# Filter spectra split by token modulo four, two items moved to the first choice of tokens, and mean squares ahead of the layers' barrier

## The reference, cut to what matters

```python
mod = (silu(cond) @ mod_w + mod_b)              # shift, scale, gate, twice: 6 x 1024 a layer
h = rms_norm(x, norm1_w) * (1 + sc1) + sh1
# filters, of the positions alone
h = sin(z @ w1 + b1); h = sin(h @ w2 + b2); h = (h @ w3 + b3) * window
# Hyena: twice
z = parts[o + 1] * bidir_fftconv(z, filt[:, 0, o], filt[:, 1, o], bias[o])   # irfft(rfft(z) * rfft(filt))
x = x + g1 * (merged @ w_o)
h2 = rms_norm(x, norm2_w) * (1 + sc2) + sh2
aff = softmax(h2 @ router_w); gate, idx = top_k(aff.T, cap)   # each of 16 experts chooses its tokens
x = x + g2 * sum over experts of (silu(xs @ w_gate) * (xs @ w_up)) @ w_down * gate
```

## Time and profile before

| | us |
|---|---|
| median of 3 runs | 2148.35 (2147.32 to 2151.87) |
| profiled execution | 2155.39 |
| its span | 2153.6 |

### The profile page before, as it was taken

One profiled execution on the slowest core, in us unless ns is written; L12 is line 12 of the kernel. 1 busy time (PEld: TensorE's weight loads), 2 busy tenths in 40 slices (PEclk: granted clock), 3 DMA queues, 4 the chain that ended last, 5 costly groups with the idle time before them and its releaser, 6 DMA issues.

```text
span 2153.6 us, 35885 instructions
## 1 busy us (share of the span) xinstructions
PE 2095.7 (97%) x13286; PEld 1707.6 (79%) x13286; DVE 1681.4 (78%) x2516; ACT 1134.5 (53%) x1798; POOL 164.2 (8%) x192
## 2 busy tenths in 40 slices
PE   8999999999999999999999999999999999999999
PEld 3449999998768997666668999999766999666666
DVE  7767878876768645999997787887777764799997
ACT  5434444324712255888884444433651225788884
POOL 1110000001001100111100000000100100111110
PEclk9999999999999999999999999999999999999999
DMA  9982433213133517999992243222413434999995
GB/s 334 329 305 87 147 136 119 83 75 117 76 118 136 171 62 294 392 382 385 382 354 98 96 147 133 98 82 76 152 42 135 159 130 159 353 378 385 385 386 216
DMA packets 76975, 435.80 MB, mean 202 GB/s; under 512 B 9228, under 2 KB 9900, under 8 KB 36381
## 3 DMA queue, kind: packets, MB, share of 16 engines
q1 hardware_dynamic: 54336, 352.87, 42.7%
q0 software_dynamic: 19024, 72.32, 10.7%
q10 hardware_dynamic: 3470, 8.64, 1.1%
HBM read 384.95 MB, written 48.84 MB: 201 GB/s over the span
## 4 chain that ended last, share of the span: by engine, by line
PE 80%; DVE 8%; ACT 4%; issue 4%; DVEq 2%; DMA 2%; ACTq 0%; POOL 0%; another core or an unknown queue 0%; POOLq 0%
PE ps L738 21%; PE ps L977 17%; PE ps L1322 9%; PE ps L1348 5%; PE ps L1326 4%; PE ps L919 3%; PE ps L1352 2%; PE ps L843 2%; PE ps L1049 2%; DMA kspec<-back 2%; PE ps L777 2%; PE ps L1174 2%; PE ps L1177 1%; PE ps L933 1%; PE ps L1102 1%
## 5 line engine op out<-in xcount | busy, mean ns | idle before, releaser
L738 PE MATMUL ps<-front_r 128*128 128x320 f32 x2432 | 417.0, 310 | 1.6 <-DVE back_r L2474 0.8
L738 PEld LDWEIGHTS ps<-front_r 128*128 128x128 f32 x2432 | 370.1, 188 | 3.0 <-DVE back_r L2474 1.4
L1420 ACT ACTIVATE front_r<-ring 128x1024 fp32r<-128x1024 f32 (+1 forms) x216 | 182.5, 845 | 261.2 <-PE ps L738 172.1
L977 PE MATMUL ps<-back_r,front_r 128*128 128x320 f32 x1728 | 265.1, 309 | 0.0
L977 PEld LDWEIGHTS ps<-back_r,front_r 128*128 128x128 f32 x1728 | 256.4, 188 | 0.0
L1420 ACT ACTIVATE back<-ps 128x512 f32<-128x512 f32 (+5 forms) x206 | 98.5, 496 | 249.6 <-PE ps L738 114.1
L977 PE MATMUL ps<-front_r 128*128 128x320 f32 x1296 | 204.7, 311 | 5.3 <-DVE back L2153 5.1
L977 PEld LDWEIGHTS ps<-front_r 128*128 128x128 f32 x1296 | 191.9, 188 | 10.4 <-DVE back L2153 9.5
L1420 ACT ACTIVATE front_r<-back 128x512 fp32r<-128x512 f32 (+2 forms) x216 | 150.1, 709 | 87.8 <-PE ps L977 35.0
L2588 DVE TENSOR_TENSOR back_r<-front,back_r 128x1024 fp32r<-128x1024 f32 x128 | 153.5, 1220 | 12.4 <-ACT back_r L1420 10.6
L1322 PE MATMUL ps<-back_r 128*80 128x512 f32 x384 | 152.3, 397 | 3.7 <-ACT back_r L1420 3.7
(11 more groups left out here) (317 smaller groups left out, 3734.8 us busy)
## 6 DMA issues: line engine op xcount, KB each, us to landing
ring<-in_stream SPq DMA_DIRECT2D x186, 1024.0 KB, 7.9
front<-in_stream SPq DMA_DIRECT2D x80, 1024.0 KB, 16.0
back<-in_stream SPq DMA_DIRECT2D x48, 1024.0 KB, 14.9
gates<-back SPq DMA_DIRECT2D x24, 640.0 KB, 3.1
back<-gates POOLq DMA_DIRECT2D x48, 320.0 KB, 3.3
kspec<-back POOLq DMA_DIRECT2D x20, 512.0 KB, 8.4
front<-kspec POOLq DMA_DIRECT2D x8, 1024.0 KB, 7.7
rows<-front ACTq DMA_DIRECT2D x10, 520.0 KB, 5.4
```

The lines of the kernel that those rows point to most:

```text
L738: mm = pe.matmul(tokh(b)[:, c0:c1], w(wp)[:, k, :], src(hp, k)[:, c0:c1], start=first, stop=last)
L977: mm = pe.matmul(ps[:, bank, 0:TH], w[:, wp, k, :], x(k), start=k == 0 and wp == 0 and x is hi and j not in (2, 6), stop=k == 3 and wp == ...
L1420: return act.activation(o, i, ACT.Copy)
```

## The change

- **Spectra.** Latent tokens are ordered by 0, 2, 1, 3 modulo 4 in effect: the even half is itself made of a transform of tokens 0 and one of tokens 2 modulo 4, over 128 frequencies only (two matmuls for each of the two parts), whose sum and difference are the even halves for kt = 0 and 1 (`keven`); the odd half stays two matmuls each. ACT copies one of the two (`ktwo`) and the prompt's spectrum; the copies of odd halves go. PE, ACT and DVE now wait for one another within a step through banks 0 to 3 of PSUM.
- **Items.** `LATE` becomes ((5, 6), (6, 4)), so `EARLY` is 27; `STEPS` tells how many a step does. In the choice of tokens three items come ahead of the transposes of the places, the others behind them, and then 4 (layer 0) or 10 (layer 1) matmuls into a bank that nobody reads. SP issues expert loads 0 to 2 instead of 0 to 5 ahead of its wait for the gather.
- **Router's shift.** `router_shift` comes behind `inverse(1)`, with one matmul that transposes the shift's columns; ACT and DVE split the result into `shift_rows`. `diag` and its 16 scalings a layer go; DVE makes `spread_rows` with two products of 96 x 1024 in the output projection and a low part of `spr`, and `add_shift` is one fp32r matmul of 512 columns over 96 partitions.
- **Between the layers.** Mean squares and root come ahead of the barrier, with 6 filler matmuls on PE.

The diff, cut to its core:

```diff
-MODS, LATE = DEPTH * N_MOD, ((5, 4), (6, 4))
+MODS, LATE = DEPTH * N_MOD, ((5, 6), (6, 4))
 EARLY = MODS - sum(sum(n) for n in LATE)
...
+        STEPS = (1,) * 10 + (1, 2, 1, 2, 2) + (1, 1, 2, 1, 2)
         def step_mods(n):
-            first = [2 + min(x, 10) + (EARLY - 12) * max(x - 10, 0) // 10 for x in (n, n + 1)]
-            return tuple(range(*first))
+            first = 2 + sum(STEPS[:n])
+            return tuple(range(first, first + STEPS[n]))
...
                 for x in range(LAP):
-                    if x == 6:
+                    if x == 3:
...
                 unit, u = n // 5, n % 5
-                b = 2 * (n % 2)
                 pe.wait_ge(f_tapsread, 5 * unit + 5)
-                if n >= 2:
-                    wait_spectrum(pe, n - 2)
                 if u == 0:
+                    pe.wait_ge(k_evac, 4 * unit)
                     for r in range(2):
-                        mm = pe.matmul(ps[:, b + r, :], cfi[:, r, :], (fa, fb)[r][:, unit % 2, 0, :],
+                        mm = pe.matmul(ps[:, r, :], cfi[:, r, :], (fa, fb)[r][:, unit % 2, 0, :], start=True, stop=True)
+                    mm.then_inc(k_ready, 1)
+                else:
+                    r, kt = (u - 1) // 2, (u - 1) % 2
+                    if r:
+                        pe.wait_ge(k_evac, 4 * unit + 1 + kt)
+                    else:
+                        pe.wait_ge(k_first, unit + 1)
+                    for t in range(2):
+                        mm = pe.matmul(ps[:, kt, :], cft[:, r, 2 + t, P * kt:P * kt + P],
+                                       (fa, fb)[r][:, unit % 2, 3 + t, :], start=t == 0, stop=t == 1)
+                    mm.then_inc(k_ready, 1)
+                if u in (0, 2):
+                    r = u // 2
+                    if unit or r:
+                        pe.wait_ge(k_evac, 4 * unit + 1 if r else 4 * unit - 1)
+                    for t in range(2):
+                        mm = pe.matmul(ps[:, 2 + t, :], cft[:, r, t, 0:P], (fa, fb)[r][:, unit % 2, 1 + t, :],
                                        start=True, stop=True)
-                else:
-                    kt, r = (u - 1) // 2, (u - 1) % 2
-                    for odd in (1, 0):
-                        for t in range(2):
-                            mm = pe.matmul(ps[:, b + odd, :], cft[:, r, 2 * odd + t, P * kt:P * kt + P],
-                                           (fa, fb)[r][:, unit % 2, 1 + 2 * odd + t, :], start=t == 0, stop=t == 1)
-                mm.then_inc(k_ready, 1)
+                    mm.then_inc(k_ready, 1)
...
                 if l:
-                    mean_squares(l, 0)
                     spread(l, 0)
...
                             for k in range(KC):
-                                mm = pe.matmul(ps[:, 7, 320 + NE * g:320 + NE * g + NE],
+                                pe.matmul(ps[:, 7, 320 + NE * g:320 + NE * g + NE],
                                                mod[:, l, 24 + k, g:g + 1].to_broadcast([P, P]), rw[:, k, :],
                                                start=k == 0, stop=k == KC - 1)
-                        mm.then_inc(r_lg, 1)
+                        pe.wait_ge(sh_hi, 2 * l + 1)
+                        pe.matmul(ps[:, 7, 0:P], shift_cols, ident[:], start=True, stop=True).then_inc(r_lg, 1)
...
                         prompt_forward()
+                    inverse(1, range(4))
+                    if o == 0:
                         router_shift()
-                    inverse(1, range(4))
                 prompt_inverse(1)
...
                     t, hf = n // 2, n % 2
-                    for i in range(4):
-                        mm = pe.matmul(ps[:, 4 + n % 2, P * i:P * i + P], spr[:, P * t:P * t + P],
-                                       diag[:, int(t > 0), 4 * hf + i, :], start=False, stop=i == 3)
-                    mm.then_inc(t_ready, 1)
+                    pe.matmul(ps[:, 4 + n % 2, :], spr[0:96, P * t:P * t + P],
+                              spread_rows[0:96, int(t > 0), 4 * hf:4 * hf + 4, :].rearrange("p i n -> p (i n)"),
+                              start=False, stop=True).then_inc(t_ready, 1)
...
                 mm.then_inc(r_affT, 1)
-                pe.wait_ge(z_ready, l * Z_IN + Z_IN)
+                pe.wait_ge(rt_lo, 3 * l + 3)
                 add_shift(0)
...
-                pe.wait_ge(r_places, l * 2 + 1)
-                apart(pe)
-                pe.transpose(ps[0:SLOTS, 0, 0:LISTS], places[:], ident[0:LISTS, 0:LISTS])
-                pe.transpose(ps[0:CAP[1], 0, LISTS:2 * LISTS], best[:], ident[0:LISTS, 0:LISTS]).then_inc(r_placesT, 1)
-                pe.wait_ge(numbers_in, l * 32 + 32)
-                pe.wait_ge(r_places, l * 2 + 2)
-                apart(pe)
-                seconds = turned[0:CAP[1], :].rearrange("p (a n) -> p a n", a=2)[:, :, 32:32 + NE]
-                pe.matmul(ps[0:CAP[1], 1, 0:2 * NE], flip, seconds, start=True, stop=True).then_inc(r_placesT, 1)
+                def turn_places():
+                    pe.wait_ge(r_places, l * 2 + 1)
+                    apart(pe)
+                    pe.transpose(ps[0:SLOTS, 0, 0:LISTS], places[:], ident[0:LISTS, 0:LISTS])
+                    pe.transpose(ps[0:CAP[1], 0, LISTS:2 * LISTS], best[:], ident[0:LISTS, 0:LISTS]).then_inc(r_placesT, 1)
+                    pe.wait_ge(numbers_in, l * 32 + 32)
+                    pe.wait_ge(r_places, l * 2 + 2)
+                    apart(pe)
+                    seconds = turned[0:CAP[1], :].rearrange("p (a n) -> p a n", a=2)[:, :, 32:32 + NE]
+                    pe.matmul(ps[0:CAP[1], 1, 0:2 * NE], flip, seconds, start=True, stop=True).then_inc(r_placesT, 1)
                 mods = late_mods(l, 1)
-                for i in mods:
+                for x, i in enumerate(mods):
+                    if x == 3:
+                        turn_places()
                     mod_rows(i)
-                    if i > mods[0]:
+                    if x:
                         mod_columns(i - 1)
                 mod_columns(mods[-1])
+                keep_busy(2, 10 if l else 4)
...
                     add_rows(1, m)
+                if l + 1 < DEPTH:
+                    pe.wait_ge(c_read, l * 8 + 6)
+                    keep_busy(2, 6)
+                    pe.wait_ge(c_read, l * 8 + KC)
+                    mean_squares(l + 1, 0)
                 end_phase(pe, l)
...
-            def spectrum_odd(n):
-                act.wait_ge(k_ready, n + 1)
-                b = 2 * (n % 2)
-                if n % 5:
-                    if n >= 2:
-                        wait_spectrum(act, n - 2)
-                    copy(kodd[:, n % 2, :], ps[:, b + 1, :]).then_inc(k_odd, 1)
-                else:
+            def spectrum_parts(n):
+                unit, u = n // 5, n % 5
+                if u == 0:
+                    act.wait_ge(k_ready, 7 * unit + 1)
                     if n >= 2:
                         act.wait_ge(k_stored[n % 2], 16 * (n // 2))
-                    copy(kout[:, n % 2], ps[:, b:b + 2, :]).then_inc(k_first, 1)
+                    copy(kout[:, n % 2], ps[:, 0:2, :]).then_inc(k_first, 1)
+                if u in (0, 2):
+                    act.wait_ge(k_ready, 7 * unit + (5 if u else 2))
+                    if unit or u:
+                        act.wait_ge(k_evac, 4 * unit + 1 if u else 4 * unit - 1)
+                    copy(ktwo, ps[:, 3, :]).then_inc(k_odd, 1)
...
                     if o:
+                        act.wait_ge(r_lg, 2 * l + 1)
+                        copy(shift_rows, ps[:, 7, 0:P]).then_inc(sh_hi, 1)
                         act.wait_ge(y_sum, l * 4 + 1)
...
                     late_add(conv_mods(l, o)[-1])
+                    if o == 0:
+                        act.wait_ge(modcol_read, conv_mods(l, o)[-1] + 1)
+                        copy(shift_cols.rearrange("p (j m) -> p j m", j=8), mod[:, l, 24:32, :].rearrange("p k g -> p (k g)")
+                             .unsqueeze(1).to_broadcast([P, 8, 16])).then_inc(sh_hi, 1)
...
                         square(2 * l + 2, m)
+                    root(l + 1, 0)
                 end_phase(act, l)
...
             def spectrum(n):
-                if n % 5 == 0:
-                    return
-                dve.wait_ge(k_odd, n - n // 5)
-                if n >= 2:
-                    dve.wait_ge(k_stored[n % 2], 16 * (n // 2))
-                even, odd = ps[:, 2 * (n % 2), :], kodd[:, n % 2, :]
-                dve.tensor_tensor(kout[:, n % 2, 0, :], even, odd, ALU.add)
-                if n % 5 % 2:
-                    ins = dve.tensor_tensor(kout[:, n % 2, 1, :], even, odd, ALU.subtract)
-                else:
-                    ins = dve.tensor_tensor(kout[:, n % 2, 1, :], odd, even, ALU.subtract)
-                ins.then_inc(k_evac, 1)
+                unit, u = n // 5, n % 5
+                if u:
+                    r, kt = (u - 1) // 2, (u - 1) % 2
+                    dve.wait_ge(k_ready, 7 * unit + (2 + u if u < 3 else 3 + u))
+                    if n >= 2:
```

(29 more changed lines are left out.)

38 lines of the change are left out of this document (19 added, 19 removed).

## The result

The changed kernel takes 2157.48 us (median of 6 runs, 2156.64 to 2161.64), the kernel before 2148.23 beside it: a ratio of 1.0042, 95% interval 1.0031 to 1.0052. It is 9 us (7 to 11) **slower**. The prediction had 2143.9 and gave slower 0.14.

A forecast was written before the change was run, and what follows sets the result against it. TensorE was taken as busy nearly throughout, with DMA near full in opening and experts and VectorE close. Terms -6.4 + 1.0 + 5.0 - 2.0 - 2.1 = -4.5 us gave 2143.9 against the median, range 2135 to 2154.

The forecast's parts named there:

- Opening, predicted -6.4: Opening: split spectra and two items fewer save 6.4 us net, from -11 to 0.
- The three groups: 99.0 becomes 91: Opening's three groups of five steps fall from 99.0 to 91 us, with 3 us taken for store waits.
- the tail, forecast +1.6: Opening's tail: two quarter combinations of 1.6 us each come ahead of the norms, one hidden: +1.6 us.
- Rival C: Opening was bound by stores, so nothing is gained there; total +1.9 us, 2150; chance 0.10.
- Router's shift, +1.0 for both layers: Convolution: small matmuls behind the second inverse add a matmul and idle time; +1.0 us, from -2.5 to +2.5.
- Choice, the gather -2.5: Choice of tokens: shift added by one matmul, last store sooner, gather issued at 840.7, 2.5 us sooner.
- Layer 0, +5: Layer 0: expert loads held behind the fifth and sixth item in SP's queue; +5 us, from -2 to +9.
- rival A: Late loads in layer 0 cost more: layer 0 +9, layer 1 +1, total +6 us, 2154; chance 0.12.
- The lateness of 12 us: Layer 0's experts: the last item lands at 1130.3 instead of about 1118.3, 12 us later, against a slack of 8.
- Layer 1, -2: Layer 1: experts start 1 us sooner, perhaps at high clock; loads 5.4 us later, under slack; -2 us, -4 to +1.
- Rival D: Choice of tokens: clock stays at half among transposes, gather no sooner; total -2.5 us, 2146; chance 0.10.
- Mean squares, -2.1: Between the layers: sums and spread at full clock cost 1.2 and 1.3 us; -2.1 us, from -3.5 to -0.5.

The follow-up runs named there:

- before_again: The kernel before once more, no edit; ratio 0.9996 to the kernel before.
- b_ms: The kernel before with mean squares and root ahead of the layers' barrier alone, with 6 fillers; ratio 0.9995 to the kernel before.
- b_shift: The kernel before with the router's shift part alone, `turn_places` and filler left out; ratio 1.0042 to the kernel before.
- a_gate: The changed kernel with six expert loads instead of three ahead of the wait for the gather, in both layers; ratio 1.0029 to the kernel before.
- a_nofill: The changed kernel without the filler matmuls behind the late items; ratio 1.0034 to the kernel before.
- a_dma: The changed kernel with layer 0's expert loads 5 and 11 of each 12 bringing half their columns (7.3 MB less); ratio 1.0014 to the kernel before.
- c_order: The changed kernel with layer 0's expert loads 0 to 2 ahead of the fifth and sixth late item in SyncE's queue; ratio 1.0013 to the kernel before.
- c_fill: c_order without filler in layer 0 and with 4 filler matmuls instead of 10 in layer 1; ratio 1.0007 to the kernel before.
- b_lesspe: The kernel before with sixteen matmuls fewer in the opening (each later spectrum's even half one matmul), VectorE's and ScalarE's work unchanged; ratio 0.9956 to the kernel before.
- a_lessdve: The changed kernel without VectorE's sums and differences of the two quarter transforms; ratio 1.0022 to the kernel before.
- c_unsplit: c_order with the spectra of the kernel before, 27 items in the opening; ratio 1.0010 to the kernel before.
- b_spectra: The kernel before with the split spectra alone, 29 items staying in the opening; ratio 1.0009 to the kernel before.
- a_items: The changed kernel with two items back in the opening, four in layer 0's choice of tokens; ratio 1.0008 to the kernel before.

## Why the prediction was wrong, point by point

**TensorE's work** fell by 16.7 us in the opening, 16.9 in the sum. It was the wrong quantity to sum.

**Opening, predicted -6.4.** The trace of the change seemed to confirm it: first projection at 155.65 for 161.28, 155 forecast. But the "before" beside it was a long execution. Over executions the spread stands at 152.2, 147.4, 149.3, 151.0 with before's opening (before, before_again, b_ms, b_shift; mean 150.0) and at 145.6, 145.4, 144.6, 151.6, 147.2, 145.1 with the changed one (changed, a_gate, a_nofill, a_dma, c_order, c_fill; 146.6): -3.4. From spread to the convolution's first transform it is 440.2 to 440.3 us in every kernel with the old spectra and TensorE's work whole, 441.3 to 442.6 with the new ones (without the quarter sums 440.5). That leaves -1.5 at the convolution. Two steps failed.

The first is "The three groups: 99.0 becomes 91". The 91 came out: 90.1 in the changed kernel (steps 5 and 10 at 43.02 and 69.46 below, step 15 at 99.83, tail at 133.14), 91.6 on average over the six. The 99.0 did not hold: it was a long execution's, and the three others with before's opening take 94.7, 94.3 and 95.8 (mean of the four 95.9). So the groups gained 4.4 us, not 8. The two items make about half of it (three executions with the old spectra and 27 items take 93.5 on average), and the split the other half (four with the new spectra and 29 items, 93.7).

```profile
43.02 0.49 PE L827 MATMUL ps<-b,rows 40*128 40x512 f32 x2
...
69.46 0.50 PE L827 MATMUL ps<-b,rows 40*128 40x512 f32 x2 [0.68 <-DVE back L2037]
...
99.83 0.49 PE L827 MATMUL ps<-b,rows 40*128 40x512 f32 x2
...
133.14 1.96 PE L842 MATMUL ps<-front,cfi 128*128 128x512 f32 x4 [1.71 <-DVE back L2058]
```

The terms inside the 91 were partly wrong and made up for each other. Group one was to gain nothing, as VectorE's; it fell from 27.9 to 26.4 us with the split, to 25.4 with TensorE's relief alone (b_lesspe), and to 24.8 with both (a_lessdve): TensorE bound it before, and VectorE in part after. Groups two and three were to have VectorE over 90% busy. It is at 18.01 of 20 us from 80 to 100, but at 15.75 and 12.98 in the two stretches of 20 us behind; without the quarter sums they are only 2.5 us shorter together than on average in the six. What binds them stays open.

The second is the tail, forecast +1.6. It takes 19.1 us with the old spectra (23.4 in c_unsplit, with its long store wait) and 20.9 to 22.6 with the new ones: +1.8 to +3.5, +2.6 on average. The prediction saw the cause, but took it into its 3 us for the groups: ScalarE's prompt copy waits for a store, the quarter's copy stands behind it, VectorE behind that, and TensorE behind both.

```profile
137.57 1.51 ACT L1446 ACTIVATE back<-ps 128x1024 f32<-128x1024 f32 x2 [7.18 <-DMA kspec<-back]
...
139.18 0.69 DVE L2062 TENSOR_TENSOR back<-ps,back 128x512 f32<-128x512 f32 x1 [5.87 <-ACT back L1446]
...
138.74 1.96 PE L851 MATMUL ps<-front,back 128*128 128x512 f32 x4 [1.71 <-ACT back L1446]
```

In a_gate and a_nofill this wait is 3.8 and 3.7 us and the tail 20.9. So the split gains 2.3 us in the groups and gives them back from the tail on, which is why b_spectra and c_unsplit show no gain, while TensorE's relief alone gave 9 us in the times and VectorE's alone 4. Rival C (nothing gained, stores) was nearer, as to the tail. In total the stores are waited for no longer than before: ScalarE waits 14.3 us for them in the changed kernel, VectorE and ScalarE 15.8 together in the first execution of before.

**Router's shift, +1.0 for both layers.** The order of events was as forecast: inverse at 619.07, then the small matmuls (626.04, 3.64 us), then the transform. From the convolution's first transform to the first turned token twelve executions with the new shift take 231.1 us in layer 0 and 231.4 in layer 1 on average, eight with the old one 230.5 and 231.3: +0.7 for both. Single ones scatter by 4 us, so that is no more than consistent.

**Choice, the gather -2.5.** Right in itself: released by the indices, 2.4 us sooner relative to the work before it. What failed is what the prediction gave it in layer 0 and 1: the rows are turned no sooner, since the gather's landing takes 8.3 us among late items and expert loads (layer 0) and the filler takes 7.3 us, not the estimated 4.3 (layer 1): the estimate took it at full clock, and it was granted 0.50 until 1848. The Trainium skill ("DMA: Bandwidth & Descriptors", Queues, rings and completion order) says that a DMA engine goes round its queues packet by packet. The trace agrees as far as the gather doesn't wait for the whole backlog: it lands in 8.3 us, at 845.1, while the three expert loads that were issued 4.3 us ahead of it take 15.1 us (median), until about 848. But its time doubled from 4.1 us beside them, which the prediction didn't price.

**Layer 0, +5.** The mechanism was right: queue held, DMA engines idle, waits for landings in the experts. What it didn't see is that the three loads behind the gather would do the same in layer 0 without the block (a_items). Its size was +6.3 (338.8, 339.1, 337.7 and 338.5 with the change's layer 0, mean 338.5; 332.4, 331.3, 331.7, 333.1, 332.2 and 332.5 with the old one, 332.2), nearly 1 us of mean squares already taken off. So it lies between the forecast and rival A's +9. The lateness of 12 us came out at about 11, an estimate: the last load was issued at about 1102 and the last two take 23.8 us (median), so it lands 306.5 us after the first turned token, for 295.1 before. Of these the slack took 4 to 5 rather than the 8 that the sum granted.

**Layer 1, -2.** The sign was wrong. Measured +1.0 (six executions with three loads ahead of the gather and 10 fillers average 330.8, eight with the old layer 1 average 329.8). The step that failed is the start of the experts, "1 us sooner": the filler, at half clock for most of its time, took more than the gather's gain, and the first row is turned 26.4 us after the first token, for 24.7 and 25.2. The loads behind the gather cost nothing in the changed kernel, as forecast (from the first turned row to the end 304.8 against 305.6 and 306.6), but the slack is nearly used up: in a_nofill, whose rows start 2.5 us sooner, the experts wait for loads. Rival D, half clock among the transposes, didn't come about (the clock is 0.89 in both kernels between 815 and 830, and 1.00 in the changed kernel between 823 and 829), though b_shift shows it at once when TensorE is left without work. The Trainium skill ("TensorE: Matmul & The Clock Gate", Part 4: PE-mode transpose) has transposes not counting as busy; here ten turns, all transposes but one matmul each, were followed by a late item at 1.07 us, full clock (829.19 in layer 0, 1833.50 in layer 1). By that rule the item should have come at half clock, as it does in b_shift; for this mix the measurement decides otherwise.

**Mean squares, -2.1.** -1.4 to -1.9. The sums cost what was forecast (1.25 us); the spread took 1.35 in b_ms, for 1.3, and 1.78 in the changed kernel.

The sum over these is -1.5 (opening) + 0.7 + 6.3 + 1.0 - 0.7 (what of the mean squares lies behind the spread) = +5.8 us. The times say +9 (7 to 11), and +6 (4 to 8) for its near twin a_gate. Of the 13.7 us between the forecast and the times, 4.9 are in the opening, 3.0 in layer 1, and 2.7 in layer 0 with the mean squares. Some 3 us stay unplaced; single traces of stages that vary by 2 to 5 us don't settle them.

## What to carry to other kernels

Price a moved transfer by the stretch in which the DMA engines would run dry, not by its own time: a 1 MB item at the head of an in-order queue that waits for a free slot holds everything behind it, and in a stage that was full of transfers to its end, as here, that time didn't come back. If removing one cause leaves the waits, look for a second that is enough by itself. Before taking work off the busiest engine add up what the same edit gives the second busiest, and try each relief alone. Take the starting value of a sum from several executions: here one long one was worth half of the forecast gain. And when an edit makes TensorE finish early in a chain, ask what it does until the next result comes: here a gap of 4.19 us cost its clock as well.

## What the runs showed of the hardware

- The time from issue to landing of a 1 MB load isn't told by the rate: 16.8 us in before, 26.9 in the changed kernel, 17.7 with fewer bytes, all at a DMA share of 1.0 and at 382 to 387 GB/s or, with fewer bytes, 377 to 383 in layer 0's experts. It follows what is outstanding: landing time times rate gives some 6 and 10 loads of 1.05 MB (estimate).
- The opening of the same program took 147.4 or 152.2 us, with single waits for a 512 KB store of up to 4.8 us in the one and 3.9 in the other; kernels differ less than this.
- After 4.19 us without work TensorE was at half clock for the whole of the next late items (1.93 for 1.07 us). After 2.97 us of waiting in a_nofill the first expert began so too, and in layer 0 of the changed kernel it did after waits of only 0.57 and 1.86 us (0.63 instead of 0.39 us a matmul for 3.4 us). With 7.3 us of filler up to the first rows it didn't, but most of the filler was at half clock.
